# Seventeen instead of sixteen gate/up pairs by seven half-size products, with other loads and sums in front of them

## The reference

```python
    hf = rms_norm(x, norm_ffn[l])
    gate, up = jnp.split(hf @ w_ffn_in[l], 2, axis=-1)
    x = x + (jax.nn.silu(gate) * up) @ w_ffn_out[l]
return rms_norm(x, norm_final)
```

## Time and profile before

| | |
|---|---|
| median of 3 runs | 1569.22 us (1568.54 to 1569.37) |
| the profiled execution | 1569.12 us |
| its span, first to last instruction | 1567.3 us |
| mean granted clock of TensorE | 0.998 of full speed |
| TensorE busy | 99% of the span |
| DVE, ACT, POOL busy | 64%, 44%, 4% |

### The profile page before, as it was taken

The page is one execution under the profiler, slowest core; times in us unless marked ns, Lnnn a source line. Parts: engine busy times, 40 slices in busy tenths (PEclk is TensorE's granted clock), DMA queues, the critical chain, the costliest instruction groups (busy, mean ns, idle before and its releaser), DMA issues.

```text
span 1567.3 us, 20924 instructions
## 1 busy us (share of the span) xinstructions
PE 1551.4 (99%) x7916; PEld 1315.4 (84%) x7916; DVE 1004.7 (64%) x1605; ACT 693.0 (44%) x1161; POOL 68.2 (4%) x58
## 2 busy tenths in 40 slices
PE   9999999999999999999999999999999989999998
PEld 7877777888888888888888888888888889989987
DVE  6776878666644545357786545465655889848735
ACT  5455776643322222264444334344444445524414
POOL 0000000020000000040000010010002000000002
PEclk9999999999999999999999999999999999999999
DMA  5333232342222322223442232334123223332322
GB/s 193 125 102 99 84 93 76 101 136 100 95 98 91 107 95 94 95 94 114 132 130 65 75 134 88 115 122 148 54 83 106 94 95 109 108 108 82 113 83 74
DMA packets 54035, 160.99 MB, mean 103 GB/s; under 512 B 6960, under 2 KB 8368, under 8 KB 53808
## 3 DMA queue, kind: packets, MB, share of 16 engines
q1 hardware_dynamic: 53632, 159.14, 31.0%
q10 hardware_dynamic: 304, 0.52, 0.1%
HBM read 148.11 MB, written 2.10 MB: 96 GB/s over the span
## 4 chain that ended last, share of the span: by engine, by line
PE 95%; DVE 2%; DMA 1%; ACT 1%; issue 1%; DVEq 0%; SPq 0%; ACTq 0%
PE G L1230 73%; PE SC L1230 7%; PE TP L1230 6%; PE O L1230 4%; PE M L1230 3%; PE TP L1653 1%; PE TP L1599 1%; DMA RAW<-in_f 1%; DVE WL L2274 0%; DMA GN<-in_gains 0%; PE TP L1702 0%; ACT WH L1740 0%; ACT MGh L1740 0%; DMA RAW<-in_fg 0%; DVE WTl L2274 0%
## 5 line engine op out<-in xcount | busy, mean ns | idle before, releaser
L1230 PE MATMUL G<-XGh,WH 128*128 128x512 f32 x984 | 388.6, 395 | 0.0
L2274 DVE TENSOR_TENSOR WL<-RAW,WH 128x1024 fp32r<-128x1024 f32 (+2 forms) x277 | 302.8, 1097 | 131.5 <-ACT WH L1740 131.1
L1230 PE MATMUL G<-XGh,WL 128*128 128x512 f32 x984 | 383.6, 390 | 0.0
L1230 PE MATMUL G<-XGl,WH 128*128 128x512 f32 x984 | 383.2, 389 | 0.0
L1740 ACT ACTIVATE WH<-RAW 128x1024 fp32r<-128x1024 f32 (+2 forms) x283 | 256.9, 913 | 152.9 <-PE G L1230 108.7
L1230 PEld LDWEIGHTS G<-XGh,WH 128*128 128x128 f32 x984 | 184.8, 188 | 41.3 <-issue 3.8
L1230 PEld LDWEIGHTS G<-XGh,WL 128*128 128x128 f32 x984 | 184.7, 188 | 39.3
L1230 PEld LDWEIGHTS G<-XGl,WH 128*128 128x128 f32 x984 | 184.9, 188 | 36.3
L1230 PE MATMUL G<-MGh,WH 128*128 128x512 f32 x372 | 145.0, 390 | 0.0
L1230 PE MATMUL G<-MGl,WH 128*128 128x512 f32 x372 | 144.7, 389 | 0.0
L1230 PE MATMUL G<-MGh,WL 128*128 128x512 f32 x372 | 144.7, 389 | 0.0
(11 more groups left out here) (420 smaller groups left out, 2759.8 us busy)
## 6 DMA issues: line engine op xcount, KB each, us to landing
RAW<-in_up SPq DMA_DIRECT2D x32, 512.0 KB, 3.2
RAW<-in_dn SPq DMA_DIRECT2D x32, 512.0 KB, 3.2
RAW<-in_fg SPq DMA_DIRECT2D x22, 512.0 KB, 4.6
RAW<-in_g SPq DMA_DIRECT2D x16, 512.0 KB, 3.2
RAW<-in_f SPq DMA_DIRECT2D x16, 512.0 KB, 3.6
X<-in_x SPq DMA_DIRECT2D x16, 256.0 KB, 4.4
RAW<-in_q SPq DMA_DIRECT2D x8, 512.0 KB, 3.3
RAW<-in_k SPq DMA_DIRECT2D x8, 512.0 KB, 3.4
```

The source lines that it names most:

```text
L1230: return e.matmul(dst, st, mv, start=start, stop=stop, skip_group_check=True)
L2274: return e.tensor_tensor(dst, src, hi.bitcast(F32), ALU.subtract)
```

## The change

- `DIRECT` becomes 5: pair 5 is now by seven products too, so there are five plain pairs and 17 of the other kind.
- The preparation of the activation sums starts a new `kt` every four half tiles of plain work (before: every five), since there is one plain pair less.
- For the first pair of the new kind (`ADDED` = 1), `t1` and `t3` are no longer made by DVE. SP loads `b11` and `b12` to their places in `T`, and POOL (step `fetch_add`) adds `b12` and `b22` onto them by accumulating DMAs, 64 partitions each, four in all. `tile_sum` 0 and 2 fall away for this pair.
- These loads are issued early: they stand at place 7 of the fetches (`EARLY`), behind the load of gate tile 3. The load of `b22` is a fetch of its own, for every pair.
- The loads of `f0` and `f1` have a fourth landing place, tiles 4 and 5 of `T` (`raw_tile(3)`), in the order of `PLACES`. `f2` starts with place 2 instead of 0.

```diff
@@ -86,9 +86,10 @@
 
-DIRECT = 6
+DIRECT = 5
 SLOTS, AHEAD = 10, 6
-SUM_AT = (0, 1, 2, 5)
+SUM_AT, ADDED, EARLY = (0, 1, 2, 5), 1, 7
+PLACES = (0, 3, 1, 2, 0, 2, 0, 1)
 HALF_S = S // 2
@@ -228,12 +229,24 @@
                 new = n - 2 < DIRECT or n in (16, 17)
-                out.append(("sums", n, 2, max(behind, held.get(2, 0)) if new else behind))
+                behind_2 = max(behind, held.get(2, 0)) if new else behind
+                if new and n % 2 == 0:
+                    behind = max(behind, held.get(3, 0))
+                if n == DIRECT:
+                    out.insert(EARLY, ("sums", n, 2, out[EARLY - 1][3]))
+                else:
+                    out.append(("sums", n, 2, behind))
+                out.append(("b22", n, 2, behind_2))
                 out.append(("pair", n, side, max(behind, held.get(side, 0))))
                 held[side] = q + 7
+                if side == 0:
+                    held[3] = q + 7
                 last_pair = q + 7
             elif name != "st" and part == 0:
-                third = (len(self.units) + n_plain) % NRAW if name in ("fg", "fu") else n % NRAW
+                if name in ("fg", "fu"):
+                    third = (len(self.units) + n_plain) % NRAW
+                else:
+                    third = PLACES[n] if name != "f2" else (n + 2) % NRAW
                 out.append((name, n, third, max(held.get(third, 0), last_pair if third == 2 else 0)))
@@ -249,6 +262,9 @@
             self.put("fetch", self.fetched)
+            name, f = self.fetches[self.fetched][:2]
+            if name == "sums" and f < DIRECT + ADDED:
+                self.put("fetch_add", f)
             self.fetched += 1
@@ -265,9 +281,9 @@
             if name == "st" and j in SUM_AT:
-                if (f, j) == (DIRECT, 0):
-                    self.settle(self.rounded)
-                self.put("tile_sum", f, SUM_AT.index(j))
+                i = SUM_AT.index(j)
+                if f >= DIRECT + ADDED or i in (1, 3):
+                    self.put("tile_sum", f, i)
             self.put("item_hi", self.rounded)
@@ -719,7 +735,7 @@
                         for kind in kinds:
-                            self.later(2 + 5 * kt + n, kind, kt)
+                            self.later(2 + 4 * kt + n, kind, kt)
             self.pair(f)
@@ -943,6 +959,10 @@
         T_SUM = (F[:, 0, :], F[:, 1, :])
+
+        def raw_tile(third):
+
+            return RAW[:, third, :] if third < NRAW else T[:, 4:6, :].rearrange("p a s -> p (a s)")
 
@@ -1072,16 +1092,19 @@
-        d_b12, d_b22 = d_x[0:2], d_x[2:4]
+        d_b12, d_b22, d_b11 = d_x[0:2], d_x[2:4], d_x[4:6]
+        LOADED = (*d_raw, d_x[6])
+        t1_added, t3_added = ([sem(f"{n}{i}") for i in range(ADDED)] for n in ("t1_added", "t3_added"))
+        SUMMED = tally("tile_sum")
...
-        RAW_LOADS, n = {}, [sum(1 for v in range(len(units)) if v % NRAW == third) for third in range(NRAW)]
+        RAW_LOADS, n = {}, [sum(1 for v in range(len(units)) if v % NRAW == third) for third in range(NRAW)] + [X_LOAD // 16]
...
-            if name != "sums":
+            if name not in ("sums", "b22"):
@@ -1147,11 +1170,14 @@
                             e.wait_ge(prep_dve, PREP_DVE["s_lo", 3])
+                        if TURN7[n] < ADDED:
+                            e.dma_start(b["t1"], a["fg"][n][:, 0:S]).then_inc(d_b11[n % 2], 16)
                         e.dma_start(b["t3"], a["fu"][n][:, 0:S]).then_inc(d_b12[n % 2], 16)
-                        e.dma_start(b["b22"], a["fu"][n][:, S:2 * S]).then_inc(d_b22[n % 2], 16)
+                    elif name == "b22":
+                        e.dma_start(b_tiles(n)["b22"], a["fu"][n][:, S:2 * S]).then_inc(d_b22[n % 2], 16)
                     else:
                         c = 768 if name == "f2" else 1024
-                        e.dma_start(RAW[:, third, 0:c], a["fg" if name == "pair" else name][n]).then_inc(d_raw[third], 16)
+                        e.dma_start(raw_tile(third)[:, 0:c], a["fg" if name == "pair" else name][n]).then_inc(LOADED[third], 16)
                 elif kind == "stack":
@@ -2145,21 +2171,27 @@
-                            e.wait_ge(t_sum, 4 * TURN7[n] + 1)
+                            if TURN7[n] < ADDED:
+                                e.wait_ge(t1_added[TURN7[n]], 32)
+                            else:
+                                e.wait_ge(t_sum, SUMMED["tile_sum", n, 0])
...
-                            e.wait_ge(t_sum, 4 * TURN7[n] + 2)
+                            e.wait_ge(t_sum, SUMMED["tile_sum", n, 1])
...
-                            e.wait_ge(t_sum, 4 * TURN7[n] + 3)
+                            if TURN7[n] < ADDED:
+                                e.wait_ge(t3_added[TURN7[n]], 32)
+                            else:
+                                e.wait_ge(t_sum, SUMMED["tile_sum", n, 2])
...
-                            e.wait_ge(t_sum, 4 * TURN7[n] + 4)
+                            e.wait_ge(t_sum, SUMMED["tile_sum", n, 3])
...
-                        src = RAW[:, third, part * S:part * S + c]
-                        e.wait_ge(d_raw[third], 16 * RAW_LOADS[name, n])
+                        src = raw_tile(third)[:, part * S:part * S + c]
+                        e.wait_ge(LOADED[third], 16 * RAW_LOADS[name, n])
@@ -2256,6 +2288,15 @@
                     e.tensor_tensor(T[:, 0, :], T[:, 0, :], COS, ALU.mult).then_inc(r_cos, 1)
+
+                elif kind == "fetch_add":
+                    f = arg[0]
+                    b, n = b_tiles(f), TURN7[f]
+                    for tile, loaded, added, more in (("t1", d_b11[f % 2], t1_added[n], slice(0, S)),
+                                                      ("t3", d_b12[f % 2], t3_added[n], slice(S, 2 * S))):
+                        e.wait_ge(loaded, X_LOAD + 16)
+                        for r in (slice(0, P // 2), slice(P // 2, P)):
+                            e.dma_start(b[tile][r, :], a["fu"][f][r, more], accum_op=ALU.add).then_inc(added, 16)
 
@@ -2839,21 +2880,24 @@
                             e.wait_ge(i_lo, taken("st", f - 2, 0))
-                            e.wait_ge(t_sum, 4 * n - 6)
-                        elif n == 1:
-                            e.wait_ge(prep_dve, PREP_DVE["s_lo", 3])
+                            e.wait_ge(t_sum, SUMMED["tile_sum", f - 2, 1])
                         e.wait_ge(d_b12[f % 2], X_LOAD + 16 * (n // 2 + 1))
...
                     elif i == 1:
-                        e.wait_ge(t_sum, 4 * n + 1)
+                        if n < ADDED:
+                            e.wait_ge(t1_added[n], 32)
+                        else:
+                            e.wait_ge(t_sum, SUMMED["tile_sum", f, 0])
                         e.wait_ge(d_b22[f % 2], X_LOAD + 16 * (n // 2 + 1))
...
                     elif i == 2:
-                        e.wait_ge(t_sum, 4 * n + 2)
+                        e.wait_ge(t_sum, SUMMED["tile_sum", f, 1])
                         e.tensor_tensor(b["t3"], b["t3"], b["b22"], ALU.add).then_inc(t_sum, 1)
                     else:
-                        e.wait_ge(t_sum, 4 * n + 3)
+                        if n < ADDED:
+                            e.wait_ge(d_raw[f % 2], 16 * RAW_LOADS["pair", f])
+                        e.wait_ge(t_sum, SUMMED["tile_sum", f, 3] - 1)
                         e.tensor_tensor(b["t4"], b["t2"], b["b21"], ALU.add).then_inc(t_sum, 1)
```

## The result

| | before | changed |
|---|---|---|
| median | 1569.37 us (9 runs) | 1564.83 us (9 runs, 1563.78 to 1566.43) |
| ratio | | 0.9972, 95% interval 0.9963 to 0.9982 |
| profiled execution | 1569.12 us | 1564.32 us |
| its span | 1567.3 us | 1562.5 us |

The change makes the kernel 4.5 us faster, 0.28%. The forecast was 1562.8 with a range of 1560.1 to 1566.5. The median lies inside the range, 2.0 us above the forecast.

What follows compares the result with a forecast made beforehand. TensorE, busy 1551.4 of 1567.3 us, bounds the kernel, so only fewer or shorter matmuls or its standstills can save time. Gains 0.8 + 3.2 + 2.45 = 6.4 us give 1562.8 against the median; range 1560.1 to 1566.5.

Steps and rivals of the forecast that it cites:

- rival 1: First pair of seven products: the clock falls after the shorter standstill too, up to 1.5 us more, 1564.3; chance 0.20.
- rival 2: First pair as late as before, by pair 6's late load or DVE backlog; (d) gives nothing, 1566.0; chance 0.14.
- rival 3: Gaps before `f0` and `f1` stay: load 2 blocks ACT or load 1 is not early enough; 1565.2; chance 0.06.
- rival 4: The first gap vanishes altogether, if TensorE needs less than counted: 1560.2; chance 0.05.
- (a): TensorE: a plain pair of 10.88 us becomes seven products of 10.09 us, gain 0.8 us.
- (b): Activation sums on DVE fit beside five plain pairs: 10.5 us a round against 10.88, no backlog at 1256.47.
- (c): First pair's `t1`, `t3` by accumulating DMAs on POOL: 32 us of cover, costed at nothing; DVE's 3.23 us load wait goes.
- rival 5: Accumulating DMAs land late, perhaps as POOL's descriptors wait for DVE; slower, 1574.2 if landing at 1262; chance 0.05.
- (d): First gap at `one_out` shrinks from 4.24 to 2.55 us, full clock after it; gain 3.2 us.
- (e): Fourth landing place for loads of `f0` and `f1` removes the gaps before them; gain 2.45 us.
- (f): Separate fetches of `b22` in the steady part: same three DMAs per pair, same order on SP; nothing.

Runs made afterwards that it cites:

- again_b: The changed kernel itself, unchanged, run a third time for its profile alone: 1564.02 us for its one execution.

## Why the prediction was right, and where its size was off

The direction and the parts were right, and so is the range; but the range was wide enough to hold rivals 1 to 4 as well. The forecast itself, 1562.8, was missed by 2.0 us, and its own signs say why: it named a clock below 0.9 behind the gap as the mark of rival 1, and the clock was 0.83. One other sign failed without harm: the accumulating DMAs had landed by 1236.2, not before 1235.

**(a) The shorter pair.** Right: pairs by seven products start 10.08 us apart, 0.8 saved.

**(b) DVE keeps up.** Right. `s_lo` of the last round ended at 1255.3 against a forecast of 1255.1, and the released evacuation came at 1256.58 against 1256.47; the 0.1 of it is TensorE's own start, which was 0.1 later. The last remainder in front of that evacuation started at 1255.91 and took its usual 0.60, so DVE was free at 1256.51, 0.07 us ahead: there was no backlog and next to no margin. Five half tiles apart and DVE-made sums both show it too. One reading of the kernel before was too simple: behind its wait of 3.23 us DVE did not run without a pause, it waited three more times for ACT (0.70, 0.62 and 0.70 us), and of the 3.23 us 1.67 were left at the last `fu`.

**(c) The accumulating DMAs cost nothing.** Right: of 32 us of cover some 21 were used. The step undersold them: without them the kernel is not faster at all. The rule of the Trainium skill ("SBUF — State Buffer", "two separate sides") that was weighed as rival 5 was not put to the test here. It speaks of two-port instructions; all that DVE ran beside the additions were tensor_tensor and scalar_tensor_tensor, and beside these, with DVE 92% busy from 1240 to 1250, the late additions landed in 3.0 to 4.6 us, the early ones in 3.2 to 4.2. No run put another kind of DVE instruction beside them.

**(d) The rest of the first gap.** The chain was right: `t2` of the second pair at 1262.39 against 1262.26, TensorE back at 1264.64 against 1264.5, 2.58 us lost against 2.55. The step that failed is the choice of the full clock after it. In the profiled execution the clock fell and took 1.59 us, so the pair gave 1.67 instead of 3.2. That is rival 1, to which I had given 0.20; it came in four of the six profiles with a gap of 2.42 or 2.48 us. With the clock up, the same kernel took 1563.09, with it down 1564.02 and 1564.32. The forecast took the one value for which the traces gave no ground over the other (no fall at 1.13, a fall at 4.08), and for this size of gap they show both.

**(e) The fourth place.** The mechanism was right, and in the profiled pair of executions the size too: 1.39 and 1.05 us, nothing lost in front of `f0` and `f1`. In the profile with the place taken back the two gaps were smaller, 0.55 and 0.66 us, and the medians have 1.5 us; whether the size of 2.45 was too large for the usual execution stays open.

**(f)** Right, nothing.

The sum for the profiled executions: 0.8 + 1.67 + 1.39 + 1.05, less 0.11 for TensorE's later start, is 4.8, and 1569.12 - 1564.32 = 4.8. The forecast of 6.4 was too large by the clock (1.5) and that start. For the median, 4.5 us, the 0.3 beyond that is within the spread of executions. Rivals 2, 3, 4 and 5 did not occur; what brings the time of rival 4 is not less work but another place of `one_out`.

## What to carry to other kernels

Where engines work through one list in order, look at the gap's releaser and ask what stands in front of it in its queue: here four steps of each pair, moved forward in the list, were worth nearly as much again as the whole change (3.9 us against 4.5). A wait in the middle of a queue that is 90% busy is carried on as a backlog to the next deadline: of 3.23 us 1.67 were left before, and beside one plain pair less all of 3.34. And a standstill of some 2.4 us on TensorE should be priced with a chance of a slow stretch behind it: 1.5 us, in four of six profiles here.

## What the runs showed of the hardware that I had not expected

- With the same standstill of 2.42 us the granted clock of the ten microseconds around it was 0.83 in three profiles and 1.00 in two; one program showed both (0.83, 0.83 and 1.00). After gaps of 1.35 and 1.55 us it stayed up; after the 2.89 us of the run with the sums five apart, which had a longer standstill just ahead of it, it was 0.83.
- The fall has no fixed place behind the standstill. In the changed kernel it came 1.0 us after TensorE had started again (1265.6), in its third profile (`again_b`) 0.7, with three landing places 0.2, and in the kernel before, after 4.08 us, at the restart itself. In the two longest standstills (4.71 us with the sums on DVE, 5.84 us with the sums five apart) it came before the restart. The first microsecond of the changed kernel and the one around the restart of the kernel before:

```profile
1264.64:1265.64 1.00, 1.00 (x8) 1.00 (x9) 0.97 (x4) 0.99 (x2) 0.00 (x0) 1.00 1.05 369
```

```profile
1277.00:1278.00 1.00, 0.93 (x4) 0.93 (x5) 0.97 (x3) 1.00 (x3) 0.00 (x0) 0.57 0.65 211
```

- Executions of one program differ by 2.7 us between the fastest and slowest of nine of the changed kernel, and by 2.0 among five where no gap is left. In the three profiles of the changed kernel the fall (1.5 us) and the start of this layer (0.6 us apart) account for all of it; for the executions without a profile it stays open.
- An accumulating DMA of 64 partitions by 2 KB issued by POOL landed in 3.2 to 4.2 us (3.0 to 4.6 in the run with late ones), and POOL started the next one only 3.3 to 4.9 us after the one before (3.5 to 4.6 in the changed kernel), though each is in its row for only 0.8 to 1.0 us and the two halves write different partitions. Why is open; no run tried it.
